# Stage boundaries of a decoder layer: fused scale and shift, residual on VectorE, and the next stage's first third ahead of two means

## What is computed

```
a = rmsnorm(x, g0) * (1 + mod1) + mod0
x = x + 0.5 * mod2 * rmsnorm(swiglu(a, w_gu[0], w_down[0]), g1)
a = rmsnorm(x, g2) * (1 + mod4) + mod3
x = x + mod5 * rmsnorm(token_mixer(a), g3)
a = rmsnorm(x, g4) * (1 + mod7) + mod6
x = x + 0.5 * mod8 * rmsnorm(swiglu(a, w_gu[1], w_down[1]), g5)
```

## Time and profile before

| | us |
|---|---|
| three runs | 2806.73, 2808.88, 2809.81 (median 2808.88) |
| profiled execution, its own time | 2809.11 |
| its span, first to last instruction | 2807.4 |
| PE busy | 2626.4 (94%) |
| DVE, ACT, POOL busy | 921.1, 651.0, 1262.0 |

### The profile page before, as it was taken

How to read it: one execution, slowest core, us unless ns; L and a number is a source line. 1 busy time by engine, 2 the same in 40 slices (tenths; PEclk the granted TensorE clock), 3 DMA queues, 4 the chain that set the end, 5 groups by cost and what they waited for, 6 DMA issues and landing times.

```text
span 2807.4 us, 49834 instructions
## 1 busy us (share of the span) xinstructions
PE 2626.4 (94%) x19658; PEld 1801.6 (64%) x19658; DVE 921.1 (33%) x1380; ACT 651.0 (23%) x1396; POOL 1262.0 (45%) x949
## 2 busy tenths in 40 slices
PE   7999999999968989999986999999959999999998
PEld 3666666666648944677754666666636666666665
DVE  2323222310275343445521541222462223222014
ACT  3311111100143233665420011111341111110012
POOL 2378777843342331333333884344324344344341
PEclk9999999999989955999997999999989999999999
DMA  6133333321101431000043332111101111112111
GB/s 235 36 99 91 97 97 97 101 70 41 36 23 39 147 107 44 1 1 2 1 113 99 99 98 60 49 46 55 38 23 53 52 51 46 52 53 60 41 41 61
DMA packets 298365, 179.47 MB, mean 64 GB/s; under 512 B 8847, under 2 KB 288773, under 8 KB 298176
## 3 DMA queue, kind: packets, MB, share of 16 engines
q1 hardware_dynamic: 282780, 156.15, 18.9%
q0 software_dynamic: 3840, 11.54, 1.4%
q10 hardware_dynamic: 11620, 10.04, 1.1%
HBM read 170.81 MB, written 11.10 MB: 65 GB/s over the span
## 4 chain that ended last, share of the span: by engine, by line
PE 86%; DVE 6%; ACT 4%; issue 2%; DMA 1%; SPq 0%; POOLq 0%; ACTq 0%; POOL 0%; DVEq 0%
PE banks L224 23%; PE banks L225 23%; PE banks L226 23%; PE banks L1924 4%; PE banks L1560 2%; PE banks L1793 2%; PE banks L1899 2%; ACT pair L552 1%; DVE rs L627 1%; PE banks L320 1%; PE banks L1922 1%; ACT ahi L555 1%; PE banks L2212 1%; PE banks L2137 1%; DVE y L644 1%
## 5 line engine op out<-in xcount | busy, mean ns | idle before, releaser
L224 PE MATMUL banks<-ahi,whi 128*128 128x344 f16 x2784 | 865.7, 311 | 24.0 <-ACT sg L964 14.4
L225 PE MATMUL banks<-alo,whi 128*128 128x344 f16 x2784 | 865.7, 311 | 0.0
L226 PE MATMUL banks<-ahi,wlo 128*128 128x344 f16 x2784 | 865.3, 311 | 0.0
L215 POOL TENSOR_SCALAR stage<-stage 128x1024 f32<-128x1024 f32 (+1 forms) x248 | 273.9, 1105 | 954.2 <-PE banks L226 885.5
L220 POOL TENSOR_TENSOR wlo<-stage,whi 128x1024 f16<-128x1024 f32 (+1 forms) x248 | 543.7, 2192 | 20.6
L224 PEld LDWEIGHTS banks<-ahi,whi 128*128 128x128 f16 x2784 | 273.7, 98 | 161.4 <-issue 17.8
L226 PEld LDWEIGHTS banks<-ahi,wlo 128*128 128x128 f16 x2784 | 273.9, 98 | 136.4
L225 PEld LDWEIGHTS banks<-alo,whi 128*128 128x128 f16 x2784 | 273.7, 98 | 133.6 <-issue 0.6
L224 PE MATMUL banks<-hhi,whi 128*128 128x344 f16 x1056 | 326.3, 309 | 3.4 <-DVE hlo L1031 3.4
L225 PE MATMUL banks<-hlo,whi 128*128 128x344 f16 x1056 | 326.3, 309 | 0.0
L226 PE MATMUL banks<-hhi,wlo 128*128 128x344 f16 x1056 | 326.3, 309 | 0.0
(11 more groups left out here) (312 smaller groups left out, 3555.0 us busy)
## 6 DMA issues: line engine op xcount, KB each, us to landing
stage<-in_w_ffn_gu_dram SPq DMA_DIRECT2D x88, 512.0 KB, 3.8
stage<-in_w_ada_dram SPq DMA_DIRECT2D x56, 512.0 KB, 3.8
stage<-in_w_ffn_down_dram SPq DMA_DIRECT2D x32, 704.0 KB, 4.5
stage<-in_w_in_dram SPq DMA_DIRECT2D x38, 512.0 KB, 3.9
first<-in_w_ada_dram SPq DMA_DIRECT2D x4, 2048.0 KB, 12.7
xrow<-in_x_prompt_dram ACTq DMA_DIRECT2D x8, 512.0 KB, 7.1
stage<-in_phi_w_dram SPq DMA_DIRECT2D x8, 512.0 KB, 4.2
ring<-in_state_win_kv_dram SPq DMA_DIRECT2D x16, 256.0 KB, 3.3
```

The source lines that it names most:

```text
L215: pool.tensor_scalar(st, st, WS, 1.0, ALU.mult, ALU.mult).then_inc(slab_scaled, 1)
L224: pe.matmul(out, w_hi, a_hi, start=start, stop=False)
L225: pe.matmul(out, w_hi, a_lo, start=False, stop=False)
L226: return pe.matmul(out, w_lo, a_hi, start=False, stop=stop)
```

## The change

In every boundary:

- `apply` and `shifted` (which takes the place of `affine`) work chunk by chunk for all thirds: DVE forms (x * scaleA) * rs in one `scalar_tensor_tensor`, ACT adds the shift and rounds to `ahi` in one activation, DVE forms (work + shift) - ahi in one `scalar_tensor_tensor`. The float32 result of scale and shift is no longer written. The buffers are three or four single chunks (`work`).
- DVE adds all 8 chunks of the residual; GpSimd only splits slabs.
- On PE the x mean of third 0 moves ahead (into the middle of the first output group of third 2, or after it), and the x mean of third 1 moves behind work of the next stage. `pe_late` says after which group of third 0 each late mean stands: y mean of third 2 after the first, x mean of third 1 after the second, x mean of third 2 after the fourth.
- Third 2 of `shifted` and the last reciprocal and `apply` move behind third 0 of the next stage (second feed-forward) or to its head (mixer).
- In the mixer, column blocks 0 and 1 are taken together by thirds: tiles 0 and 1 of both blocks, then 2 to 4 of both, then 5 to 8 of both.
- Into the second feed-forward, one sum of squares of third 2 (`tail["dve"](dve, 2, 1)`) now stands ahead of the product y * rs of third 1.

```diff
 def x_mean(pe, j):
     if post is not None:
-        pe.wait_ge(S("ysq"), b("ysq") - tail["units"] * (2 - j))
+        pe.wait_ge(S("rms_sqrt"), b("rms_sqrt", (1, 2, 5)[j]))
...
+            def means():
+                y_mean(pe, 1, summed(1))
+                if pre is not None:
+                    x_mean(pe, 0)
...
             if nu == 2:
-                tail["pe"](pe, 2, 0, lambda: y_mean(pe, 1, summed(1)))
+                tail["pe"](pe, 2, 0, means)
             else:
                 tail["pe"](pe, 2, 0)
-                y_mean(pe, 1, summed(1))
-                tail["pe"](pe, 2, 1)
-            if pre is not None:
-                x_mean(pe, 0)
-            for u in range(1 if nu == 2 else 2, nu):
+                means()
+            for u in range(1, nu):
                 tail["pe"](pe, 2, u)
-            if pre is not None:
-                pe.wait_ge(S("ysq"), b("ysq") - 1)
-                x_mean(pe, 1)
...
+        def shifted(act, j):
...
+            for c in range(KD):
+                act.wait_ge(S("tmp_w"), b("tmp_w", j * KD + c + 1))
+                act.activation(ahi[:, c, lo_:hi_], work(j, c)[:, 0:hi_ - lo_], ACT.Identity,
+                               bias=shift[:, c, 0:1]).then_inc(S("a_hi"), 1)
...
+        def add(dve, j):
+            lo_, hi_ = third(j)
+            xc = x[:, :, lo_:hi_]
+            dve.wait_ge(S("y_scaled"), b("y_scaled", j + 1))
+            dve.tensor_tensor(xc, xc, y[:, :, lo_:hi_], ALU.add).then_inc(S("x_new"), 1)
...
+            def low(c):
+                dve.wait_ge(S("a_hi"), b("a_hi", j * KD + c + 1))
+                dve.scalar_tensor_tensor(out=alo[:, c, lo_:hi_], in0=work(j, c)[:, 0:w], scalar=shift[:, c, 0:1],
+                                         in1=ahi[:, c, lo_:hi_], op0=ALU.add, op1=ALU.subtract).then_inc(S("a_lo"), 1)
...
+            for c in range(KD):
+                if c >= depth(j):
+                    dve.wait_ge(S("a_lo"), b("a_lo", j * KD + c - depth(j) + 1))
+                dve.scalar_tensor_tensor(out=work(j, c)[:, 0:w], in0=x[:, c, lo_:hi_], scalar=scaleA[:, pre, c, 0:1],
+                                         in1=rs[:, j, 0:w], op0=ALU.mult, op1=ALU.mult).then_inc(S("tmp_w"), 1)
+                if c >= 2:
+                    low(c - 2)
+            low(KD - 2)
+            low(KD - 1)
...
+            inverse(dve, 1, 1)
+            if nu == 4:
+                tail["dve"](dve, 2, 1)
+            scaled_y(dve, 1)
+            add(dve, 1)
...
+        pe_late, act_late, dve_late = {}, None, None
+        if post is None:
+            pe_late = {0: lambda pe: x_mean(pe, 2)}
+        elif pre is not None:
+            pe_late = {0: last_y_mean, 1: lambda pe: x_mean(pe, 1), 3: lambda pe: x_mean(pe, 2)}
+            act_late, dve_late = lambda act: shifted(act, 2), last_apply
...
# ffn, first pass, on PE; ACT and DVE have the same with act_late and dve_late after third 0
-                            if j == 0 and v == 0 and late_y:
-                                late_y(pe)
-                            if j == 0 and v == late_after:
-                                late_x(pe)
+                            if j == 0 and v in pe_late:
+                                pe_late[v](pe)
...
# mixer, column blocks 0 and 1 on PE
+            for j, tiles in enumerate((range(0, 2), range(2, 5), range(5, 9))):
+                for n in range(2):
+                    pe.wait_ge(slab_split, sa + n + 1)
+                    for t in tiles:
+                        if t > 0:
+                            pe.wait_ge(S("a_lo"), a_ready[j])
+                        tile_product(pe, n, t, t // 4, n == 0 and t == 0)
+                    if j == 0:
+                        pe_late[n](pe)
+                if j == 0:
+                    pe_late[3](pe)
```

More of the change, by code:

```diff
@@ new lines, in squares @@
+        def squares(act, j):
+            lo_, hi_ = third(j)
+            if post is None:
+                x_ready(act, j)
+            else:
+                act.wait_ge(S("x_new"), b("x_new", j + 1))
+            for half in range(2):
+                chunks_ = slice(4 * half, 4 * half + 4)
+                act.activation(squares_of(j)[:, chunks_, :], x[:, chunks_, lo_:hi_],
+                               ACT.Square).then_inc(S("xsq"), 1)
+        def shifted(act, j):
+            lo_, hi_ = prompt_cols(j)
+            act.wait_ge(S("x_mean"), b("x_mean", 1))
+            if post is not None:
+                act.wait_ge(S("x_new"), b("x_new", 2 if j == 0 else 3))
+            for c in range(KD):
+                act.wait_ge(S("tmp_w"), b("tmp_w", j * KD + c + 1))
+                act.activation(ahi[:, c, lo_:hi_], work(j, c)[:, 0:hi_ - lo_], ACT.Identity,
+                               bias=shift[:, c, 0:1]).then_inc(S("a_hi"), 1)
@@ L509, in _ @@
         @block.scalar
         def _(act):
[L511 to L556, removed]
@@ L568, in _ @@
                 if pre is not None:
-                    squares(0)
+                    squares(act, 0)
                 if nu == 2:
-                    root_y(1)
+                    root_y(act, 1)
+                    if pre is not None:
+                        root_x(act, 0)
                     tail["act"](act, 2, 0)
@@ L610, in _ @@
+            shifted(act, 1)
+            root_x(act, 2)
+            shifted(act, 2)
+        if post is not None and pre is not None:
             @block.gpsimd
             def _(pool):
[L612 to L620, removed]
+                for v in range(4):
+                    split_slab(pool, at("slab"), 0, v, KD * P)
@@ L707, in _ @@
             if post is None:
-                inverse(0, 0)
+                inverse(dve, 0, 0)
                 first_mods_dve(dve)
@@ new lines, in _ @@
+            for u in range(nu):
+                tail["dve"](dve, 0, u)
+            tail["dve"](dve, 1, 0)
+            inverse(dve, 0, 0)
+            if nu == 4:
+                tail["dve"](dve, 1, 1)
+            scaled_y(dve, 0)
+            add(dve, 0)
+            for u in range(1 if nu == 2 else 2, nu):
+                tail["dve"](dve, 1, u)
+            if nu == 4:
+                tail["dve"](dve, 2, 0)
+            inverse(dve, 1, 1)
+            if nu == 4:
+                tail["dve"](dve, 2, 1)
```

372 lines of the change are left out of this document (168 added, 204 removed).

## The result

The changed kernel takes 2765.66 us (median of 4 runs, 2763.88 to 2767.42) against 2808.99 for the kernel before: the ratio is 0.9847, 95% interval 0.983 to 0.9864, a gain of 43.3 us. The profiled execution has a span of 2763.8.

What follows compares the result with a forecast made beforehand. PE, busy 94%, was taken to bound the kernel, with 72 us of waits to win. Gains of 5.9 + 15.5 + 12 + 1.0 = 34.4 from 2809.1 gave 2775 us, range 2768 to 2794.

Steps and rivals of the forecast that it cites:

- The four places that were to pay: Gains forecast into the first feed-forward 5.9, into the mixer 15.5, into the second feed-forward 12, at the end 1.0 us.
- 3 to 5: Into the second feed-forward, DVE stands still some 3 to 5 us ahead of the moved sum of squares.
- rival D: Fused operations on two float32 SBUF inputs need two DVE passes, 0.88 each; 52 us lost, so 2827; chance 0.07.
- 16 x 0.54 = 8.7 for a third: DVE's fused chunks at 0.52 plus 0.02 between two; a third takes 8.7 instead of 9.8, worth 1.1 us.
- The sign that I had set: Fused lines on DVE at 0.52 as forecast; 0.6 would say rival B, 0.88 rival D.
- rival B: Part is given back to the clock and other costs in the boundaries: gain 25.3 us, so 2784; chance 0.24.
- the clock was kept as I took it: Into the first feed-forward, full granted clock behind the shorter wait, worth 2.6 of 5.9 us; without it 3.3.
- costed at nothing: GpSimd's adds leaving its queue, earlier splits and SP's transfers had no term; cover fails at about 2 us a meeting.
- third 0 comes about as before: Into the mixer, third 0 was given no gain or loss in time.
- what I named as cover: GpSimd and DVE two-input work taking turns (4.12 beside DVE's 1.95) was cited for splits ahead of time meeting DVE's work.
- 15.5: Gain into the mixer: third 2 8.1 us earlier, 8 tiles behind it instead of 13; between 12 and 17.3.
- 12: Gain into the second feed-forward: third 2 ends 3.1 us earlier, four groups behind it instead of six; 9 to 16.

Runs made afterwards that it cites:

- `sum_back`: Changed kernel with the one sum of squares of third 2 back behind the residual of third 1, into the second feed-forward: 2761.79 us (0.9833).
- `unfused`: Changed kernel with order and residual kept, but each chunk formed as before, without fused operations: 2784.18 us (0.9906).
- `order_only`: Changed kernel with chunks formed as before and GpSimd's residual adds put back, so only the order differs from before: 2791.51 us (0.9932).
- `changed_again`: The changed kernel run and profiled once more, with no edit: 2764.63 us (0.9843).
- `gpsimd_add`: Changed kernel with GpSimd's 3 of 8 residual chunks and their place among the splits put back: 2770.72 us (0.9856).
- the three edits: Changed kernel with `sum_back`, `mean_early` and third 2's reciprocal ahead of third 0's Silu products into the second feed-forward; together 2755.72 us (0.9812).
- `mean_early`: Changed kernel with third 2's last output group taken over earlier, into the mixer and into the second feed-forward: 2762.99 us (0.9838).

## Why the prediction was wrong

**What held.** The four places that were to pay do so, in the order of size forecast. The end gave 1.1 for 1.0, the first feed-forward 5.7 for 5.9 (by luck, as shown below). The waits for squares over 10 us and the one of 10.4 for a Silu are gone. The standstill that the change adds is there: 4.87 us for "3 to 5", and `sum_back` shows its net price, 3.7. The fused operation does not take two passes, so rival D is out: the line stands at

```profile
L652 DVE SCALAR_TENSOR_TENSOR pair<-x,scaleA,rs x48: 558/572/2318, 63.5 to 833.0; 128x344 f32<-128x344 f32 x32, 128x336 f32<-128x336 f32 x16
```

and the sentence of the Trainium skill ("Vector Engine (DVE) Microarchitecture Reference", section "7. Points that are easy to get wrong") on halved throughput is not borne out here: 0.558 at the least, where a plain product took 0.500 in `unfused`.

**The step that failed first: "16 x 0.54 = 8.7 for a third".** DVE by time, third 1 into the mixer:

```profile
816.75 1.55 DVE L652 SCALAR_TENSOR_TENSOR pair<-x,scaleA,rs 128x344 f32<-128x344 f32 x3
818.21 0.57 DVE L644 SCALAR_TENSOR_TENSOR alo<-pair,mods,ahi 128x344 f16<-128x344 f32 x1
818.70 0.57 DVE L652 SCALAR_TENSOR_TENSOR pair<-x,scaleA,rs 128x344 f32<-128x344 f32 x1
819.19 0.57 DVE L644 SCALAR_TENSOR_TENSOR alo<-pair,mods,ahi 128x344 f16<-128x344 f32 x1
...
823.09 1.55 DVE L644 SCALAR_TENSOR_TENSOR alo<-pair,mods,ahi 128x344 f16<-128x344 f32 x3
824.86 2.30 DVE L615 RECIPROCAL rs<-rs 128x344 f32<-128x344 f32 x1 [0.23 <-DVE alo L644]
```

One lasts 0.57, but the next starts 0.49 later: neighbours overlap where nothing makes one wait for the other. A third takes 7.9 (816.75 to 824.64), 0.8 less than predicted. I had added a gap to a duration, where starts must be subtracted. The sign that I had set misled in the same way: a row of 0.57 was nearer to the 0.6 that should speak for rival B. The trace of before could have told it: two instructions of 0.88 together read 1.66. Into the first feed-forward it shows alone: counted from PE's small products ahead of the stage, PE's wait for the Silu ended at 98.76 - 59.30 = 39.5 before and at 95.47 - 61.03 = 34.4 after:

```profile
61.03 1.16 PE L331 MATMUL banks<-cst,y 9*128 9x9 f32 x16 [0.68 <-ACT y L269]
...
95.47 0.31 PE L226 MATMUL banks<-ahi,whi 128*128 128x344 f16 x1 [0.65 <-ACT sg L939]
```

That is 5.0 earlier, not 3.3, and the clock was kept as I took it. In `order_only` it ended at 99.30 - 59.22 = 40.1, so the fused form is worth 5.6 there, and the new order costs 0.6. The stage's gain of 5.7 hides it, since in that profile 1.4 were lost ahead of it: the first x mean took 6.26 instead of 4.87 behind a wait of 1.98, the very gap behind which I had read a full clock. In `changed_again` the stage gained 8.3.

**The second: "costed at nothing" and "third 0 comes about as before".** I let the residual on DVE cost 1.2 at each inner boundary and credited it with 1.5, the wait for squares in third 1's 11.3, and with 1.0 at the end. `gpsimd_add` prices it at 2.5 to 2.7 into the mixer, by the start of third 2's tiles, and at 2.6 into the second feed-forward (the 4.0 of the mixer's stage has 1.4 of clock in it). With the adds back, the end of third 0 into the mixer comes 46.4 after the first y mean instead of 45.0 (47.3 in the kernel before), and the reciprocal of y mean 2 at 51.7 instead of 49.6; then squares of third 2 wait 2.3 for GpSimd. The reciprocal in the changed kernel, then in `gpsimd_add` with the add and the squares:

```profile
805.82 2.30 DVE L615 RECIPROCAL rs<-rs 128x344 f32<-128x344 f32 x1 [1.58 <-ACT rs L526]
...
805.24 2.30 DVE L624 RECIPROCAL rs<-rs 128x344 f32<-128x344 f32 x1 [2.25 <-ACT rs L526]
...
810.94 4.12 POOL L620 TENSOR_TENSOR x<-x,y 128x1032 f32<-128x1032 f32 x1 [16.17 <-DVE y L637]
...
815.15 2.59 ACT L543 ACTIVATE sqx<-x 128x1376 f32<-128x1376 f32 x2 [2.27 <-POOL x L620]
```

So what I named as cover, turns between GpSimd and DVE, was a cost in the kernel before that the change removes. By its length the 4.12 is such a turn: GpSimd's two-input step of a split, 1024 columns, takes 2.13 where DVE has no two-input work beside it (844.40 in the profile after), and here DVE's add of 1.95 goes first; all 8 chunks on DVE take 3.0. I took that reciprocal as 5.6 and 6.1 earlier than before; it is 7.9 and 8.0, and with the adds back 5.8 and 6.2. Into the second feed-forward third 0 was to come 2 later; it ended 0.6 earlier (49.2 instead of 49.8), and with the adds back 1.7 later.

The turns with the splits stay; the prediction named them and gave them no term in the sum. Third 0 into the mixer, formed while GpSimd splits slabs (until 796.0), takes 15.8 (785.38 to 801.16), where third 1, with GpSimd idle, takes 7.9. No run was made to move the splits.

The two steps close the account. Third 2 ends 12.0 earlier into the mixer (80.2 after the first y mean instead of 92.2), not 8.1: 2.3 by that reciprocal and 1.6 by two faster thirds. Into the second feed-forward it ends 5.7 earlier, not 3.1: 1.9 by the reciprocal and 1.6 by the thirds, less 0.9 that is left over; DVE stood idle for 3.2 there while ACT loaded its table, which I had not counted.

**The third is the clock**, taken as 1.7 lost into the mixer and 1.9 into the second feed-forward. Into the second feed-forward nothing was lost behind the wait of 2.9: 14.0 us for four groups. Into the mixer the profile after had 1.3 less loss than taken, `changed_again` 1.4 more. With this, 15.5 + 3.9 + 1.3 - 0.5 (a wait for the rotation's data) is 20.2 for 20.1, and for `changed_again` 17.5 for 17.2; 12 + 2.6 + 1.9 is 16.5.

The range failed with the sum: its low end took the best end of each gap and of the clock, but the fused operation's lower bound was the value that I took, and the turns had no end on the side of a gain.

## What to carry to other kernels

Price a run of instructions by the distance of their starts, in a stretch where nothing waits; a duration plus a gap counts an overlap as a cost. When work leaves another engine for the one on the critical chain, look in the chain for the waits that it caused there before calling the move neutral. And read an edit at the end of the wait that it is to shorten, not by the length of its stage in one profile: at the second feed-forward the three edits moved that mark by 3.7, 1.8 and 4.4 and together by 9.5, while the stage lengths say 3.7, 0.2, -0.2 and 7.8, with the clock behind short waits in between.

## What the runs showed of the hardware

Behind the same short wait of PE the granted clock may fall or not. The wait of 2.2 for `hlo` in the second feed-forward stands in all 13 profiles; in three of them the clock was 0.98 over 100 us with it (1.7 us lost), in ten 1.00. Behind the wait of 1.98 into the first feed-forward the first x mean took 4.87 in ten profiles and 6.26, 6.56 and 7.90 in three. Behind a wait of 2.9 it was 1.00 in the changed kernel and `sum_back`, and 0.84 over 19 us in `mean_early`. Such a wait therefore carries some 1.4 to 3 us either way, which is as large as most single edits here. In the mixer, products that nobody reads, put in the place of waits of 2.5 and 3.4, kept the clock at 1.00 over the 8 tiles behind them in two kernels. Why it falls in one execution and not in another was not tried.
